# Expert stage of a hybrid layer: half of a pair's output blocks move between the gate and the up products of the next pair

## What is computed

```python
gate = jnp.minimum(xb @ w_gate[e] + b_gate[e], SWIGLU_LIMIT)
up = jnp.clip(xb @ w_up[e] + b_up[e], -SWIGLU_LIMIT, SWIGLU_LIMIT)
h = gate * jax.nn.sigmoid(SWIGLU_ALPHA * gate) * (up + 1.0)
return h @ w_down[e] + b_down[e]
...
y = y.reshape(n_slots, D) * slot_w[:, None]
out = jax.ops.segment_sum(y, slot_tok, num_segments=T + 1)[:T]
```

## Time and profile before

| | us |
|---|---|
| median of 3 runs | 2785.42 (2783.54 to 2788.27) |
| profiled execution, its own time | 2782.88 |
| its span (first to last instruction) | 2781.2 |
| PE (TensorE matmuls) busy | 2729.4 (98% of the span) |
| DVE (VectorE) busy | 1399.4 (50%) |
| ACT (ScalarE) busy | 441.7 (16%) |
| mean granted TensorE clock | 0.995 of full speed |
| DMA, mean | 235 GB/s |

### The profile page before, as it was taken

How to read it: one execution, slowest core, us unless ns; L and a number is a source line. 1 busy time by engine, 2 the same in 40 slices (tenths; PEclk the granted TensorE clock), 3 DMA queues, 4 the chain that set the end, 5 groups by cost and what they waited for, 6 DMA issues and landing times.

```text
span 2781.2 us, 55107 instructions
## 1 busy us (share of the span) xinstructions
PE 2729.4 (98%) x23447; PEld 2093.3 (75%) x23447; DVE 1399.4 (50%) x2802; ACT 441.7 (16%) x766; POOL 67.0 (2%) x115
## 2 busy tenths in 40 slices
PE   8999999999999999999999999999999999999997
PEld 8999999999999988888899999843444444444442
DVE  6777777777777847777675562221111211112114
ACT  3121221221221121110010000131112111121110
POOL 1000000000000000000000000000000000000000
PEclk9999999999999999999999999999999999999999
DMA  7333243342243633344477556489999999999996
GB/s 222 93 122 122 93 152 112 103 152 92 93 153 101 174 122 122 124 140 133 156 213 223 170 171 223 151 360 384 429 428 428 428 428 427 428 428 427 428 428 238
DMA packets 304841, 654.83 MB, mean 235 GB/s; under 512 B 45233, under 2 KB 274737, under 8 KB 279537
## 3 DMA queue, kind: packets, MB, share of 16 engines
q1 hardware_dynamic: 304624, 651.61, 63.2%
HBM read 649.49 MB, written 2.10 MB: 234 GB/s over the span
## 4 chain that ended last, share of the span: by engine, by line
PE 76%; DVE 12%; DMA 5%; DVEq 3%; issue 3%; SPq 1%; ACT 0%
PE bank L751 21%; PE bank L1277 12%; PE bank L1092 10%; PE bank L1318 7%; PE bank L1261 4%; DMA arena<-in_w_up_dram 4%; PE bank L1147 4%; DVE arena L2145 4%; PE bank L1359 4%; DVE arena L2147 3%; DVE arena L2149 3%; PE bank L698 2%; DVE arena L1953 1%; PE bank L827 1%; PE bank L848 1%
## 5 line engine op out<-in xcount | busy, mean ns | idle before, releaser
L751 PE MATMUL bank<-arena 128*128 128x128 f32 x5376 | 642.0, 277 | 0.0
L751 PEld LDWEIGHTS bank<-arena 128*128 128x128 f32 x5376 | 615.1, 192 | 11.4 <-issue 3.8
L1277 PE MATMUL bank<-arena 128*64 128x512 f32 x2048 | 447.3, 596 | 7.3 <-DMA arena<-in_w_up_dram 7.3
L1277 PEld LDWEIGHTS bank<-arena 128*64 128x64 f32 x2048 | 147.8, 138 | 304.8 <-issue 304.8
L1092 PEld LDWEIGHTS bank<-arena 128*128 128x128 f32 x2576 | 287.8, 192 | 0.1
L1092 PE MATMUL bank<-arena 128*128 128x128 f32 x2576 | 287.8, 275 | 0.0
L2492 DVE TENSOR_SCALAR arena<-bank 128x512 f32<-128x512 f32 x16 | 11.1, 692 | 449.8 <-PE bank L1277 449.8
L1013 PE MATMUL bank<-arena 128*128 128x256 f32 x1024 | 223.5, 380 | 0.0
L1013 PEld LDWEIGHTS bank<-arena 128*128 128x128 f32 x1024 | 194.0, 190 | 26.7
L1318 PE MATMUL bank<-arena 128*64 128x512 f32 x960 | 209.3, 594 | 0.5 <-ACT arena L1661 0.5
L1318 PEld LDWEIGHTS bank<-arena 128*64 128x64 f32 x960 | 67.5, 137 | 131.6 <-issue 130.9
(11 more groups left out here) (355 smaller groups left out, 2745.6 us busy)
## 6 DMA issues: line engine op xcount, KB each, us to landing
arena<-in_w_in_dram SPq DMA_DIRECT2D x72, 2048.0 KB, 9.2
arena<-in_w_gate_dram SPq DMA_DIRECT2D x64, 2048.0 KB, 28.4
arena<-in_w_up_dram SPq DMA_DIRECT2D x64, 2048.0 KB, 21.0
arena<-in_w_down_dram SPq DMA_DIRECT2D x64, 2048.0 KB, 22.9
arena<-in_w_dn_out_dram SPq DMA_DIRECT2D x16, 2048.0 KB, 8.4
arena<-in_w_glu_b_dram SPq DMA_DIRECT2D x8, 2048.0 KB, 8.3
arena<-in_w_glu_a_dram SPq DMA_DIRECT2D x8, 2048.0 KB, 8.3
arena<-in_w_mix_out_dram SPq DMA_DIRECT2D x8, 2048.0 KB, 14.2
```

The costliest lines, as they stand in the source:

```text
L751: last = mm(regions[:, 4 * bank + place % 4], left(k), right(k), start=k == 0, stop=k == KD // 2 - 1)
L1277: last = mm(ps[bank][CAP * o:CAP * o + CAP, :], xg[:, 8 * h + k, CAP * o:CAP * o + CAP], w[o][:, k], start=False, stop=h == 1 and k == 7, ...
```

## The change

Three edits, all in the expert stage, for pairs 1 to 14:
1. `scatter(i-1, 0, 4)` moves from behind `gather(i+1)` to between `sgate(i)` and `sup(i)`. Blocks 4 and 5 stay behind the gather, 6 and 7 behind `turn_hidden`. Pair 15 keeps `scatter(14, 0, 6)` behind its up products.
2. Banks 0 and 1 hold gate and up at that point, so blocks 0 to 5 take banks 2 and 3 in turn, and only blocks 6 and 7 take banks 0 and 1 (`SCATTER_BANK`). Each block from 2 to 5 waits for the addition of the block two before it; the wait for `up_taken` stands at block 6.
3. On VectorE the four `Pw` instructions move from `stake_up` to the end of `stake_gate`, and `add_scatter(i-1, 0, 4)` comes right behind `stake_gate(i)`, before `select(i+1)`.

```diff
+SCATTER_BANK = (2, 3, 2, 3, 2, 3, 0, 1)
@@ scatter
                     pe.wait_ge(y_copied, 4 * i + 4)
-                    pe.wait_ge(up_taken, i + 2)
...
                 for n in range(lo, hi):
-                    if n >= 4:
-                        pe.wait_ge(sc_taken, 8 * i + n - 3)
-                    bank = (2, 3, 0, 1)[n % 4]
+                    if 2 <= n < 6:
+                        pe.wait_ge(sc_taken, 8 * i + n - 1)
+                    if n == 6:
+                        pe.wait_ge(up_taken, i + 2)
+                    bank = SCATTER_BANK[n]
@@ sparse
+                early = 4 if more and not first else 0
                 sgate(i)
+                if early:
+                    scatter(i - 1, 0, early)
                 sup(i)
...
-                    scatter(i - 1, 0, 6)
+                    scatter(i - 1, early, 6)
@@ stake_gate, stake_up
                 dve.sem_inc(gate_taken, 1)
-
-            def stake_up(i):
-                dve.wait_ge(units_read, PER_PAIR * i + 8)
-                V.tensor_scalar(shb, ps[1][:, :], LIMIT, -LIMIT, ALU.min, ALU.max)
                 for m in range(MT):
                     for o in range(2):
                         V.tensor_scalar(Pw[:, m, o], slots1, column(possel, m, i, o), column(wt, m, i, o),
                                         ALU.is_equal, ALU.mult)
+
+            def stake_up(i):
+                dve.wait_ge(units_read, PER_PAIR * i + 8)
+                V.tensor_scalar(shb, ps[1][:, :], LIMIT, -LIMIT, ALU.min, ALU.max)
@@ the loop over pairs 1 to 14
                     stake_gate(i)
+                    add_scatter(i - 1, 0, 4)
                     select(i + 1)
                     stake_up(i)
-                    add_scatter(i - 1)
+                    add_scatter(i - 1, 4, 8)
```

More of the change, by code:

```diff
@@ L1347, in scatter @@
                     pe.wait_ge(y_copied, 4 * i + 4)
-                    pe.wait_ge(up_taken, i + 2)
                 biased = isinstance(i, int) and i == 0
-                if biased:
+                if biased and lo == 0:
                     pe.wait_ge(wtt_taken, 1)
@@ L2510, in stake_up, with add_scatter @@
                 dve.sem_inc(hb_ready, 1)
-            def add_scatter(i):
-                for n in range(8):
+            def add_scatter(i, lo, hi):
+                for n in range(lo, hi):
                     av = acc[:, n // 4, (n % 4) * 512:(n % 4) * 512 + 512]
                     dve.wait_ge(sc_done, 8 * i + n + 1)
-                    V.tensor_tensor(av, av, ps[(2, 3, 0, 1)[n % 4]][:, :], ALU.add).then_inc(sc_taken, 1)
+                    V.tensor_tensor(av, av, ps[SCATTER_BANK[n]][:, :], ALU.add).then_inc(sc_taken, 1)
             over = dve.value_load(flag[0:1, 0:1], min_val=0, max_val=1)
@@ L2524, in _ @@
                     stake_gate(i)
+                    add_scatter(i - 1, 0, 4)
                     select(i + 1)
                     stake_up(i)
-                    add_scatter(i - 1)
+                    add_scatter(i - 1, 4, 8)
                 stake_gate(PAIRS - 1)
                 stake_up(PAIRS - 1)
-                add_scatter(PAIRS - 2)
+                add_scatter(PAIRS - 2, 0, 8)
                 for n in range(4):
```

## The result

The changed kernel takes **2793.53 us** (median of 7 runs, 2791.84 to 2795.65) against 2785.42 us (7 runs, 2783.54 to 2788.27): ratio 1.0033, 95% interval 1.0023 to 1.0042. The medians differ by 8.1 us, where 10.4 us were forecast (2795.8 us, range 2784 to 2800). The ratio is taken over all runs and is not the quotient of the two medians; it amounts to 9.2 us.

A forecast was written before the change was run, and what follows sets the result against it. DMA, at 58.8 us a pair, was taken as slightly slower than PE at 57.46. PE's added 21.9 us less 11.5 of slack gave +10.4 us, so 2795.8 us, range 2784 to 2800.

The forecast's parts named there:

- PE becomes the bound: Steady pairs: new period 59.1 us, just above the 58.8 DMA needs, so PE sets the pace.
- The slack: Up to pair 15's up products: PE has lost 11.5 us to DMA, and added PE work below that costs nothing.
- The sum for a pair: Pairs 2 to 14: shapes, stall and transposes add 1.66 us a pair, 21.6 us over 13 pairs.
- shapes: Between gate, early blocks and up: two more changes of tile shape on PE, 0.35 us a pair.
- the stall: At block 2 behind the gate: PE waits for VectorE's first addition, 1.19 us a pair, bounds 0.93 to 1.4.
- the transposes: Behind the gather: only two blocks now cover ScalarE's last copy, so PE waits 0.12 us a pair, from 0 to 0.2.
- The drain of VectorE: Behind the gate's limit: 0.26 us gap from the trace; the skill's 0.42 would add 2.1 us in all, judged contradicted.
- Pair 1: Its blocks have bias products and take about twice as long, so VectorE is in time: only 0.35 us.
- The end: Pair 15: blocks wait for the first addition instead of `Pw`; the way to the transposes is equally long, 0 us.
- The first: Rival: waits for DMA hide all PE time added in the pairs, no change, 2785.4 us; chance 0.17.
- The second: Rival: pair 1's earlier blocks fill DMA's 6.7 us idle hole and later units land sooner, 2779 us; chance 0.05.
- The third: Rival: each pair's PE pause brings a lower clock, up to 24 us over 14 pairs, 2820 us; chance 0.04.

The follow-up runs named there:

- half-load runs: Each weight unit's load cut to its first half, in both kernels: kernel before 2773.03 us (ratio 0.9955), changed kernel 2794.29 us (1.0038).
- four other versions with parts of the change: Changed kernel with `Pw` behind up's limit again, 2788.3 us; with two early blocks, 2786.49; with four banks, 2786.35; with only its two banks kept, 2786.66.
- the run with pauses of 1.90 us: Changed kernel with the four `Pw` instructions run twice behind the gate's limit, with a drain between: 2823.45 us, ratio 1.0137.
- two banks only: Order of the kernel before on all engines, with blocks 0 to 5 on banks 2 and 3 in turn: 2786.66 us, ratio 1.0004.
- bias side by side: Kernel before with the bias products of pair 0's blocks issued in groups ahead of the blocks: 2777.61 us, ratio 0.9978.
- `Pw` back: Changed kernel with the four `Pw` instructions moved back behind the limit of up: 2788.3 us, ratio 1.0008.

## Why the prediction was right

*PE becomes the bound.* Right, and shown by the pair of half-load runs: without DMA the kernel before gains 12.1 us, the changed kernel nothing.

*The slack.* Worked out as 11.5 us from one profiled execution, measured 12.1 as a difference of medians (8.9 to 15.9 us by the interval) and 11.6 from pair 1 on (903.4 less 891.8).

*The sum for a pair.* 1.66 us worked out, 1.61 measured. By its terms: shapes 0.35 and 0.36, the stall 1.19 and 1.10, the transposes 0.12 and 0.15. In the stall errors partly cancelled, which is luck in a small term. The gap behind the gate's limit is 0.35 us, not 0.26. But the first addition starts 0.08 us before the end of the `Pw` row (2259.25 + 0.98 against 2260.15), and PE restarts 0.06 us behind the addition (2260.15 + 0.68 by its own row, against 2260.89), not 0.18.

*The drain of VectorE.* The Trainium skill's 0.42 us (page "VectorE: DVE Perf Modes", section "The DRAIN you can't avoid") lies 0.07 us above the measured 0.35, the 0.26 of the earlier trace rows 0.09 below it. So the prediction dismissed the page's figure too firmly: for this gap neither was better. In the kernel a `dve.drain()` and a semaphore stand behind the gate's limit, and none behind the limit of up, where the next row starts 0.08 us before the limit's ends. The median says nothing on it, the rows decide.

*Pair 1.* 0.35 us expected, 0.15 measured: its blocks change shape for their own bias products anyway, and one such change now coincides with the new one. That reason is argued, not shown.

*The end.* Equal was expected, and from the end of up to the transposes lie 2751.34 - 2744.33 = 7.01 us in the changed kernel against 7.13 before (2739.53 - 2732.40).

*The sum.* 21.1 less 12.1 is 9.0 us; the medians differ by 8.1, with an interval of 6.4 to 11.7 us. The profiled executions differ by 11.8 us of span, since the changed one reached pair 1 2.4 us later (and pair 0 too, ahead of any edited instruction). From pair 1 on they differ by 9.4 us. So the forecast of 10.4 was some 1 us high by its small terms; what is left to the 8.1 of the medians is within the noise.

*The rivals.* The first was the near one: four other versions with parts of the change, at 57.8 to 58.2 us a pair, are hidden by DMA but for 0.3 to 4.9 us from pair 1 on, which include falls of the clock and the last pair's wait. The second's mechanism is real too, but a move across one pair does not fill the hole; less work on PE does. The third's mechanism shows in the run with pauses of 1.90 us. The prediction's argument against it, that pair 0's pause of 1.60 us left the clock alone, was weaker than it looked. The same two pauses (1.59 or 1.60, then 0.46 us) stand in all twelve traces; the 64 down products behind them take 13.95 us in five, the kernel before and the changed one among them, and 15.44 to 15.65 in seven. PE's timeline, the kernel before and the one with two banks only, and a window of the latter:

```profile
1863.89 13.95 PE L1318 MATMUL bank<-arena 128*64 128x512 f32 x64 [0.46 <-ACT arena L1661]
```

```profile
1864.85 15.65 PE L1319 MATMUL bank<-arena 128*64 128x512 f32 x64 [0.46 <-ACT arena L1666]
```

```profile
1867.00:1869.00 2.00, 2.00 (x8) 0.61 (x6) 0.00 (x0) 0.00 (x0) 0.00 (x0) 0.53 1.02 434
```

In the changed kernel's 13 pairs, with pauses of 0.84 us, no fall came; the one row of 1.60 us that the prediction leaned on could not have told so. On this rival the prediction was partly lucky.

## What to carry to other kernels

When two resources run neck and neck, work out the slack of the faster one in us over the whole stage, and weigh a per-iteration cost times its count against it: here up to some 0.9 us a pair (12 us over 13 pairs) was all but hidden, and what went above it cost in full. Work moved between two phases helped here only in the last pair, where it left the time behind DMA's last delivery; in the pairs before, with the total unchanged, it gained nothing. Before blocks are given fewer banks, follow the engine that empties them from its previous instruction on: one addition is shorter than one block here, and the pause came from what stood ahead of the first addition.

## What the runs showed of the hardware beyond expectation

Pauses of PE of one and the same length, 1.90 us, each behind products, left the granted clock alone in 3 pairs and halved it for a stretch in 10, which cost 1.63 us each. Other pauses are as mixed: 1.60 us in pair 0 was followed by a fall in 7 of 12 executions, 2.06 us (two banks only) and one of 2.40 us (bias side by side) by none, another of 2.39 us in that same execution by one, and the longest, 2.60 to 2.71 us, by one each time. Pauses of 0.84 us brought none in 26 pairs of two executions, nor did two of 1.80 us ahead of pair 15's output blocks; in the same place 2.15 and 2.16 us did (two banks only, `Pw` back). So the length of a pause alone did not decide, and an added 1.07 us a pair on VectorE cost 30 us in place of the 14 worked out. What does decide is open. And four bias products of 32 rows each, in different rows and banks, took together 1.07 us (1915.22 to 1916.29), against 1.05 us for a single one between blocks in the kernel before (1913.79 to 1914.84).
